# Two split input tiles laid with 2,112 bytes from row to row instead of 2,048

## What is computed

```python
# first block, per layer l (256 tokens)
x = x + concat([y_ssd, y_sc, y_nsa]) @ w_out[l]
u = causal_dwconv(rmsnorm(x, ffn_norm_w[l]) @ ffn_w_up[l], ffn_conv_w[l], ffn_conv_b[l])
gate, val = split(u, 2)
x = x + (silu(gate) * val) @ ffn_w_down[l]

# second block, per layer: x (256 tokens) and ctx (256 tokens) go through the same weights
x  = x  + 0.5 * mx[2] * swiglu(modulate(rms_norm(x,  g), mx[0], mx[1]), ffn_w_in[layer, 0], ffn_w_out[layer, 0])
xc = xc + 0.5 * mc[2] * swiglu(modulate(rms_norm(xc, g), mc[0], mc[1]), ffn_w_in[layer, 0], ffn_w_out[layer, 0])
# then a mixer (latent attention in layer 0, windowed attention in layer 1), then a second swiglu
```

## Time and profile before

| | us |
|---|---|
| median of 3 runs | 2292.59 (2291.66 to 2293.55) |
| profiled execution: span from first to last instruction | 2290.5 |
| median less span (what lies around the span) | 2.1 |
| TensorE matmuls busy | 2266.0 (99%) |
| TensorE weight loads busy | 2012.7 (88%) |
| VectorE busy | 1699.2 (74%) |
| ScalarE busy | 950.0 (41%) |

### The profile page before, as it was taken

The page is one execution under the profiler, slowest core; times in us unless marked ns, Lnnn a source line. Parts: engine busy times, 40 slices in busy tenths (PEclk is TensorE's granted clock), DMA queues, the critical chain, the costliest instruction groups (busy, mean ns, idle before and its releaser), DMA issues.

```text
span 2290.5 us, 35253 instructions
## 1 busy us (share of the span) xinstructions
PE 2266.0 (99%) x14406; PEld 2012.7 (88%) x14406; DVE 1699.2 (74%) x2772; ACT 950.0 (41%) x1414; POOL 119.7 (5%) x85
## 2 busy tenths in 40 slices
PE   9999999999999999999999999999999999999998
PEld 8899999899998888898789888888888888989997
DVE  7989888989889858854446983884884673797774
ACT  6766545766542122235553212223321222475443
POOL 0010010200000000010001000001000001001001
PEclk9999999999999999999999999999999999999999
DMA  7355475354646545532111553553454453304543
GB/s 277 135 190 186 161 256 194 120 203 173 201 143 204 186 144 193 181 114 83 40 72 56 203 195 107 184 179 115 157 192 157 139 178 105 137 31 148 184 157 120
DMA packets 67025, 355.08 MB, mean 155 GB/s; under 512 B 7344, under 2 KB 10544, under 8 KB 43056
## 3 DMA queue, kind: packets, MB, share of 16 engines
q1 hardware_dynamic: 66304, 352.49, 44.3%
q10 hardware_dynamic: 560, 0.33, 0.0%
HBM read 351.75 MB, written 1.05 MB: 154 GB/s over the span
## 4 chain that ended last, share of the span: by engine, by line
PE 91%; DVE 6%; ACT 2%; issue 1%; DMA 0%; DVEq 0%; ACTq 0%
PE bank L555 90%; DVE sb_w_lo L2255 2%; ACT sb_w_hi L1486 1%; PE bank L1438 1%; DVE sb_products L2289 1%; ACT sb_nP L1486 0%; PE bank L1312 0%; DVE sb_nP L2951 0%; DVE sb_nP L2978 0%; DMA sb_res<-x 0%; DVE sb_mid L2859 0%; DVE sb_latP L3115 0%; DVE sb_decays L2990 0%; ACT sb_decays L1486 0%; DVE sb_mid L2860 0%
## 5 line engine op out<-in xcount | busy, mean ns | idle before, releaser
L1486 ACT ACTIVATE sb_w_hi<-sb_raw 128x2048 fp32r<-128x2048 f32 (+5 forms) x301 | 491.3, 1634 | 398.8 <-PE bank L555 394.4
L2255 DVE TENSOR_TENSOR sb_w_lo<-sb_raw,sb_w_hi 128x2048 fp32r<-128x2048 f32 (+3 forms) x280 | 564.1, 2015 | 117.8 <-ACT sb_w_hi L1486 114.0
L555 PE MATMUL bank<-sb_f_pair,sb_w_hi 128*128 128x256 f32 (+1 forms) x2090 | 523.9, 339 | 5.2 <-DVE sb_w_lo L2255 4.2
L555 PE MATMUL bank<-sb_h_hi,sb_w_hi 128*128 128x512 f32 (+1 forms) x1400 | 510.8, 365 | 0.6 <-DVE sb_w_lo L2255 0.4
L555 PE MATMUL bank<-sb_h_lo,sb_w_hi 128*128 128x512 f32 (+1 forms) x1400 | 507.3, 362 | 0.0
L555 PE MATMUL bank<-sb_h_hi,sb_w_lo 128*128 128x512 f32 (+1 forms) x1400 | 507.2, 362 | 0.0
L555 PEld LDWEIGHTS bank<-sb_f_pair,sb_w_hi 128*128 128x128 f32 x2090 | 360.3, 190 | 51.7 <-DVE sb_w_lo L2255 7.2
L2289 DVE CUSTOM_DVE_ANT_0 sb_products<-sb_raw,sb_cond,sb_params 128x1024 f32<-128x1024 f32 x280 | 360.0, 1286 | 32.9 <-DVEq L2291 16.2
L555 PE MATMUL bank<-sb_f_pair,sb_w_lo 128*128 128x256 f32 (+1 forms) x1122 | 366.1, 326 | 0.0
L555 PEld LDWEIGHTS bank<-sb_h_hi,sb_w_hi 128*128 128x128 f32 x1400 | 264.1, 189 | 42.9 <-issue 0.9
L555 PEld LDWEIGHTS bank<-sb_h_lo,sb_w_hi 128*128 128x128 f32 x1400 | 264.2, 189 | 41.2 <-issue 0.5
(11 more groups left out here) (329 smaller groups left out, 2917.0 us busy)
## 6 DMA issues: line engine op xcount, KB each, us to landing
sb_raw<-w_mod SPq DMA_DIRECT2D x144, 512.0 KB, 3.2
sb_raw<-w_l_up SPq DMA_DIRECT2D x44, 1024.0 KB, 4.8
sb_raw<-w_l_in SPq DMA_DIRECT2D x22, 1024.0 KB, 5.5
sb_raw<-w_l_down SPq DMA_DIRECT2D x32, 704.0 KB, 4.4
sb_raw<-w_m0a_up SPq DMA_DIRECT2D x22, 1024.0 KB, 4.8
sb_raw<-w_m0b_up SPq DMA_DIRECT2D x22, 1024.0 KB, 4.8
sb_raw<-w_m1a_up SPq DMA_DIRECT2D x22, 1024.0 KB, 4.8
sb_raw<-w_m1b_up SPq DMA_DIRECT2D x22, 1024.0 KB, 4.8
```

What stands on the lines that cost most here:

```text
L555: return nc.tensor.matmul(out, lhsT, rhs, start=start, stop=stop, skip_group_check=True)
L1486: return nc.scalar.activation(out, in_, func, **kw)
L2255: V.tensor_tensor(split_part(*at, w_lo[s]), landed_part(*at, raw[raw_slot(*at)]), split_part(*at, w_hi[s]).bitcast(F32), ALU.subtract).the ...
```

## The change

`h_hi` and `h_lo` get 528 floats (2,112 bytes) from row to row; only the first 512 are used, the last 16 floats of each row are never read. `h_lo` then starts 16,896 bytes behind `h_hi`, everything from `M` on moves up by 1,024 bytes, and `lat_lo` is placed so that it lies behind the fifth row again. No instruction is added, removed or moved, and no wait changes: the two programs differ in addresses alone.

```diff
 RAW_W = T + 2
+WIDE_ROW = 2 * T + 16
...
         H = bytes_at[0]
-        bytes_at[0] += 32768
-        h_wide = [sb(f"h_{n}", [P, KD, 2 * T], F32R, at=H + 16384 * i) for i, n in enumerate(("hi", "lo"))]
+        bytes_at[0] += 2 * KD * 4 * WIDE_ROW
+        h_wide = [sb(f"h_{n}", [P, KD, WIDE_ROW], F32R, at=H + KD * 4 * WIDE_ROW * i)[:, :, 0:2 * T]
+                  for i, n in enumerate(("hi", "lo"))]
         h_thin = [sb(f"hx_{n}", [P, KD, T], F32R, at=H + 8192 * i) for i, n in enumerate(("hi", "lo"))]
...
-        lat_lo = [sb(f"lat_lo{i}", [P, 3, 512], F32R, at=H + 16384 * i + 10240) for i in range(2)]
+        lat_lo = [sb(f"lat_lo{i}", [P, 3, 512], F32R, at=H + 4 * WIDE_ROW * (KD * i + 5) + 192) for i in range(2)]
```

## The result

The changed kernel takes 2308.24 us (2306.71 to 2309.48, four runs) against 2292.43 us of four runs of the kernel before: ratio 1.0066, 95% interval 1.0054 to 1.0078. Forecast were 2286.7 us and a range up to 2294. It is 15.8 us slower, and its span is 16.2 us longer.

What follows compares the result with a forecast made beforehand. TensorE, busy 99% of the span, was taken to bound the kernel through its start-to-start distances. Span 2290.5 less 5.9 gave 2284.6, and with 2.1 us around it 2286.7 us; range 2276 to 2294.

Steps and rivals of the forecast that it cites:

- What bounds the kernel: Whole span: TensorE, busy 99%; time is the sum of distances from one matmul's start to the next.
- That the starts of the moving rows set the gap: Back-to-back matmuls: where a moving row starts changes the 13.3 ns gap, mostly down, and not dependably.
- Step (1): Wide tiles, 2,112 bytes from row to row: 1.4 ns less for each of 4,200 matmuls, 5.9 us less.
- The bounds: Step (1), by averages of shifted stages: from 10.9 us less (l1_in) to 1.7 us more (m1b_up).
- The slower case: Wide-tile matmuls: unequal steps fall on the long side, 2 ns more on average, 8.4 us, 2301.0 us; chance 13%.
- The larger gain: Wide-tile matmuls: gap like l0_up's first step, 4 ns less on average, 16.8 us, 2275.8 us; chance 14%.
- Steps (2) to (4): Move of everything from `M` on, `lat_lo` with few stationary-operand matmuls, engines falling behind TensorE: no cost counted.

Runs made afterwards that it cites:

- the width runs: Kernel before with 512-column matmuls cut to 384 (wide inputs) and 448 (`f_pair`) columns, tiles at place 0, then 192 bytes later against the weights: 2196.6 and 2183.8 us.

## Why the prediction was wrong

- What bounds the kernel: right. The sum of the distances from start to start is the time, and what the change did to them came through in full (16.0 of 16.2 us).
- That the starts of the moving rows set the gap: right as far as it goes; what counts, as far as the runs go, is where they lie against the weights, and the low and high rows of one k keep the same place in the changed layout (16,896 is 66 x 256), so only one step in three changes it. The change gave 16 us and not 0, and moving the weights alone by 64 bytes gave 16 as well. By the two rules of the Trainium skill that the prediction sets beside it ("TensorE: Matmul & The Clock Gate", "Step-by-step: what each phase is for", and "SBUF — State Buffer", "Who interferes with whom"), an address would have had no price. Here the measurement decides; whether the ports are the reason no run shows.
- Step (1) failed in its term for the 3,144 matmuls of 512 columns. I wrote that the gap is 13.3 ns at both widths, "so it is a price per matmul and not per column", and took a saving seen at 256 columns, 1.4 ns, over to 512. An equal gap at one place does not say that it moves alike from there. For 512 columns the term was -1.4 ns and measured +5.0, with the sign turned; 3,144 x 5.0 is 15.7 us.
- For the 1,056 of 256 columns the step held in sign and rough size: 119.9 ns fell to 117.6, 2.3 ns where 1.4 were taken, 1.7 us less in all with what is lost at waits.
- Of the 5.0 ns, the four places alone account for 3.6: (226.7 + 228.9 + 232.4 + 233.3) / 4 = 230.3 ns against 231.7 measured, with place 64 as the h stages had it. The rest goes with the change of place between rows, which the run with only the low tile moved shows to cost by itself.
- The bounds were too narrow for the same reason. I had drawn them from the averages of three stages of 256 and 258 columns, 2.6 less to 0.4 more. The stage of 258 columns, whose gap was no better than the even one, was a sign that a shifted row need not be quicker, and I gave it little weight.
- The slower case had the right mechanism for 512 columns, the even rhythm given up and the steps on the long side. It was priced at 2 ns on 4,200 matmuls, 2301 us, and given 13%; measured were 5 ns on three quarters of them and the other sign on the rest.
- The larger gain rested on the first step of l0_up, where the low row starts 64 bytes from the high one. The changed layout has no such pair, and where the low wide tile alone was moved by 64 bytes the mean was 232.0 ns, slower.
- Steps (2) to (4) held: the move of `M` cost nothing (2292.95 us with it and with the low tile 256 bytes further), `lat_lo` nothing (230.0 and 230.1 ns), and nobody fell behind.

What stays open is why. Shown are that the placement of moving rows and weights sets the gap, that a shift of 256 bytes changes nothing, that a change of place costs too, and that the sign differs between 256 and 512 columns. Not shown is what makes a stage fall into one of two rhythms at the same place. That the moving row and the next weights collide on their way out of the memory fits these, but no run separated it from anything else, and the width runs did not give it a simple form.

## What to carry to other kernels

In a stage where the matmuls stand back to back, measure the distance from start to start over a long stretch and take off the columns; the gap that is left can move by half with where the moving rows lie against the weights (here from 13.3 to 20 ns at 512 columns and from 13.3 to 6.7 at 256). Read it stage by stage, since a mean over the run can mix two rhythms. Do not take a gain seen at one width to another: look for a row of the same width, and if there is none, let both signs stand in the range. Tiles of different widths can be given different places, which was worth half a per cent here once the wide ones were left alone. Before counting on such a gain in full, see how far the engine that feeds TensorE is from its own limit.

## What the runs showed of the hardware

- 512 columns: 226.7 ns from start to start with moving rows and weights at equal addresses modulo 256 bytes, 229 to 234 ns at the seven other multiples of 32 bytes.
- 256 columns: means of 120 ns at place 0 and 96, 114 to 119 at the others, 113.4 in l0_up with every row at 192.
- One place and width can have two steady rhythms: 113.3 or 117.8 ns (256 columns, place 192), 228.9 or 233.3 (512, place 64), 202.7 or 206.7 (448, place 0).
- The steps run in short cycles that repeat for the length of a stage: 226.7 throughout at place 0; 232, 226, 229 at place 64; 231, 236 in the up stages at place 192, whether the inputs or the weights were moved, and an even 233.3 in one later stage (850 to 960 us) with the inputs moved, with equal means.
- Each cycle read here lasts a whole multiple of 6.67 ns, the time of 16 columns at 2.4 GHz: 340 ns for 3 steps (place 192, 256 columns), 680 for 3 (place 0, 512), 687 for 3 (place 64), 1,627 for 7 (place 128), 1,640 for 7 (place 160), 2,780 for 12 (the changed kernel) and 3,480 for 15 (low tile moved by 64) are 51, 102, 103, 244, 246, 417 and 522 times that. Why is not shown.
- TensorE's clock was granted at 1.00, its upper level, in all of these stretches, so none of it is the clock.
